# One tile of the memory's keys moved ahead of attention-out, and the slot that it frees loaded first

## What is computed

```
# block 1
merged = gates[0] * (conv_out @ w_conv_out) + gates[1] * (attn_out @ w_attn_out)
x  = x + merged @ w_out
h2 = rms_norm(x, ffn_norm_g)
x  = x + hierarchical_moe(h2, ...)     # 32 experts, each (w_g, w_u, w_d) = 3 x 2 MB
# block 2 (its keys of the memory do not depend on x)
k, v = split(rms_norm_2(mem, g_mem) @ w_kv)
```

## Time and profile before

| | us |
|---|---|
| median of 3 runs (lowest, highest) | 1080.14 (1079.3, 1080.64) |
| the profiled execution, its own time | 1080.13 |
| its span in the trace | 1078.3 |
| busy in the span: TensorE, VectorE, ScalarE | 940.9, 476.3, 346.2 |
| the queue of SyncE's loads | 298.89 MB, 70.3% of 16 engines' span |

### The profile page before, as it was taken

One profiled execution on the slowest core, in us unless ns is written; L12 is line 12 of the kernel. 1 busy time (PEld: TensorE's weight loads), 2 busy tenths in 40 slices (PEclk: granted clock), 3 DMA queues, 4 the chain that ended last, 5 costly groups with the idle time before them and its releaser, 6 DMA issues.

```text
span 1078.3 us, 14213 instructions
## 1 busy us (share of the span) xinstructions
PE 940.9 (87%) x6026; PEld 678.1 (63%) x6026; DVE 476.3 (44%) x774; ACT 346.2 (32%) x558; POOL 1.3 (0%) x5
## 2 busy tenths in 40 slices
PE   6999999999978685867676766889999999999998
PEld 6968888985423141322222131379989999999986
DVE  5769878450101010010101010186865666888842
ACT  5422364131000010000000010247674736665632
POOL 0000000000000000000000000000000000000000
PEclk9999999999989897888888796999999999999999
DMA  8694410699999999999999999972244244556451
GB/s 314 221 370 151 156 40 1 257 395 416 428 421 420 424 427 426 423 429 424 428 422 430 423 427 424 405 253 78 80 154 159 79 157 140 173 179 212 157 195 40
DMA packets 76892, 300.80 MB, mean 279 GB/s; under 512 B 3745, under 2 KB 30498, under 8 KB 60194
## 3 DMA queue, kind: packets, MB, share of 16 engines
q1 hardware_dynamic: 75520, 298.89, 70.3%
q10 hardware_dynamic: 1314, 1.07, 0.3%
HBM read 298.90 MB, written 1.05 MB: 278 GB/s over the span
## 4 chain that ended last, share of the span: by engine, by line
PE 64%; DMA 28%; DVE 5%; ACT 1%; SPq 1%; issue 1%; DVEq 0%; PEldq 0%; ACTq 0%
PE bank L1288 11%; PE bank L647 9%; DMA ring<-in_w_down_e_dram 8%; DMA ring<-in_w_up_e_dram 8%; DMA ring<-in_w_gate_e_dram 8%; PE bank L970 6%; PE bank L1306 6%; PE bank L1174 3%; PE bank L1189 3%; PE bank L734 3%; PE bank L674 3%; PE bank L1081 3%; DMA qvpr<-in_w_down_e_dram 3%; PE bank L1023 3%; PE bank L853 2%; PE bank L995 2%
## 5 line engine op out<-in xcount | busy, mean ns | idle before, releaser
L970 PE MATMUL bank<-ring,big 128*32 128x512 f32 x768 | 165.2, 711 | 64.0 <-DMA ring<-in_w_up_e_dram 37.4
L970 PEld LDWEIGHTS bank<-ring,big 128*32 128x32 f32 x768 | 36.6, 127 | 185.4 <-issue 94.5
L343 DVE TENSOR_TENSOR ring_parts<-ring,ring_parts 128x2048 fp32r<-128x2048 f32 (+1 forms) x54 | 118.8, 2248 | 35.5 <-ACT ring_parts L335 35.2
L335 ACT ACTIVATE ring_parts<-ring 128x2048 fp32r<-128x2048 f32 (+1 forms) x54 | 98.7, 1880 | 48.7 <-DMA ring<-in_w_up_dram 27.0
L970 PE MATMUL bank<-qvpr,big 128*32 128x512 f32 x112 | 64.9, 735 | 23.1 <-DMA qvpr<-in_w_gate_e_dram 11.5
L1288 PE MATMUL bank<-mrg_parts,ring_parts 128*128 128x256 f32 x640 | 82.3, 281 | 0.0
L2025 DVE TENSOR_TENSOR xT<-bank,xT 128x512 f32<-128x512 f32 x32 | 22.1, 691 | 131.3 <-PE bank L1009 131.3
L1288 PEld LDWEIGHTS bank<-mrg_parts,ring_parts 128*128 128x128 f32 x640 | 78.5, 189 | 0.0
L970 PE MATMUL bank<-hs,big 128*32 128x512 f32 x128 | 68.2, 686 | 1.9 <-DMA hs<-in_w_gate_e_dram 1.1
L1979 DVE TENSOR_TENSOR big<-big,const 128x128 f32<-128x128 f32 x16 | 4.1, 290 | 139.3 <-PE bank L957 139.0
L2021 DVE TENSOR_TENSOR big<-bank,big 128x512 f32<-128x512 f32 x8 | 5.5, 691 | 131.1 <-PE bank L970 131.1
(11 more groups left out here) (347 smaller groups left out, 1573.1 us busy)
## 6 DMA issues: line engine op xcount, KB each, us to landing
ring<-in_w_gate_e_dram SPq DMA_DIRECT2D x24, 2048.0 KB, 19.2
ring<-in_w_up_e_dram SPq DMA_DIRECT2D x24, 2048.0 KB, 29.5
ring<-in_w_down_e_dram SPq DMA_DIRECT2D x20, 2048.0 KB, 21.0
ring<-in_w_in_dram SPq DMA_DIRECT2D x13, 2048.0 KB, 13.7
ring<-in_w_up_dram SPq DMA_DIRECT2D x22, 1024.0 KB, 7.1
qvpr<-in_w_down_e_dram SPq DMA_DIRECT2D x5, 2048.0 KB, 25.7
ring<-in_w_down_dram SPq DMA_DIRECT2D x5, 2048.0 KB, 7.9
ring<-in_w_out_dram SPq DMA_DIRECT2D x4, 2048.0 KB, 8.3
```

The costliest lines, as they stand in the source:

```text
L335: signal(act.activation(pairs[stage][u % 3][0][:, part], raws[stage][u % 3][:, part], ACT.Copy), stage + "_hi")
L343: signal(eng.tensor_tensor(lo[:, part], raws[stage][u % 3][:, part], hi[:, part].bitcast(F32), ALU.subtract), name)
L970: mm = pe.matmul(bank[part][CAP * j:CAP * j + CAP, :], xeT[:, c, CAP * j:CAP * j + CAP], w[j][c], start=(c == 0), stop=(c == DC - 1))
```

## The change

Tile 3 of the keys is computed with tiles 0 to 2, ahead of attention-out. Tile 4 takes its old place behind the norm's sum. Nothing stands any more between the transposes and the counting of positions. The semaphore of slot 4, which the first matmul behind tile 3 tells, is so told by the first matmul of attention-out, and SyncE's queue has unit 4 (into slot 4) as its first load. ScalarE's moves follow the tiles, and the list of banks follows the new order.

```
-    ... some("kx", 0, 3) + some("ao", 0, 8) + some("wo", 0, 8)
-    uses += [("n2", 0)] + some("kx", 3, 4) + some("rt", 0, 2) + some("h2t", 0, 4) + some("kx", 4, 5)
+    ... some("kx", 0, 4) + some("ao", 0, 8) + some("wo", 0, 8)
+    uses += [("n2", 0)] + some("kx", 4, 5) + some("rt", 0, 2) + some("h2t", 0, 4)
...
             def first_turn():
+                load_unit(0, 4)
                 load_unit(0, 1)
...
                 load_spare(0)
-                for u in (4, 7):
-                    load_unit(0, u)
+                load_unit(0, 7)
                 sp.wait_ge(S["keys_read"], 1)
                 load_spare(1)
...
-            mem_keys((0, 1, 2))
+            mem_keys((0, 1, 2, 3))
...
             norm_sum(("n2", 0), sq)
-            mem_keys((3,))
+            mem_keys((4,))
...
             freed.append(used[HS])
-            mem_keys((4,))
             pe.wait_ge(S["member"], 1)
...
             # ScalarE
-            for m in range(3):
+            for m in range(4):
                 move(("kx", m), ...)
             arrive(act, ("gt", 15))
             round_out(1)
...
             root(("n2", 0))
-            for m in range(3, 4):
+            for m in range(4, 5):
...
-            for m in range(4, 6):
+            for m in range(5, 6):
```

More of the change, by code:

```diff
@@ L106, in psum_plan @@
     uses += some("gt", 8, 13) + [("mu", 0), ("gt", 13), ("var", 0), ("gt", 14), ("gt", 15)] + some("s1", 4, 8) + some("aT1", 0, 2) + some("co", 0, 4) + some("aT1", 2, 4) + some("mT", 0, 4) + some("o1", 0, 4)
-    uses += some("co", 4, 6) + [("nmem", 0)] + some("on", 0, 2) + some("co", 6, 8) + some("kx", 0, 3) + some("ao", 0, 8) + some("wo", 0, 8)
-    uses += [("n2", 0)] + some("kx", 3, 4) + some("rt", 0, 2) + some("h2t", 0, 4) + some("kx", 4, 5)
+    uses += some("co", 4, 6) + [("nmem", 0)] + some("on", 0, 2) + some("co", 6, 8) + some("kx", 0, 4) + some("ao", 0, 8) + some("wo", 0, 8)
+    uses += [("n2", 0)] + some("kx", 4, 5) + some("rt", 0, 2) + some("h2t", 0, 4)
     uses += some("pos", 0, 2) + [("cnt", 0)] + some("kx", 5, 6)
```

## The result

The changed kernel takes 1087.39 us, the median of six runs (1085.44 to 1088.63), beside 1080.14 for the kernel before (six runs, 1079.3 to 1081.58). The ratio is 1.0067, with a 95% interval of 1.0056 to 1.0078: 7.25 us slower. Timed a second time, beside other kernels, it took 1086.91, ratio 1.0056 (1.0043 to 1.0069). What was expected of the second timing was 1087.4 again, with times spread over 3 us or more if the low clock were a matter of chance; its five times lie between 1086.03 and 1087.46. The forecast was slower by 4.45 us, 1084.6, with its own range of 1083.4 to 1086.0 and an 8-in-10 range of 1082.3 to 1087.5. The sign and the place are right. The time lies outside the first range and only 0.1 us inside the second; the size is near rival 1's, 1087.1.

The account below looks back on a forecast made before the run. It took one DMA stream to bound the experts' stretch. Unit 7, requested 9.0 us later, would land at 247.4 instead of 242.96; those 4.45 us on 1080.13 give 1084.6 us, range 1083.4 to 1086.0 (8 in 10: 1082.3 to 1087.5).

Parts of the forecast that it names:

- rival 1: Clock low through the counting and tile 5; unit 7 goes at 239.2; delay 7.0 us, 1087.1 us; chance 0.12.
- The stream is the bound, and lateness passes whole: Experts' stretch: one DMA stream bounds it; moving its end moves the kernel's end by as much; 4.45 us pass whole.
- By as much: Behind the experts' stream: whatever moves the stream's end moves the kernel's end by the same amount.
- The tile ahead of attention-out fills no wait: Three tiles already cover attention-out's wait to within 0.5 us; the fourth puts everything dependent back by 3.45 us.
- The pause, and slot 6 told by tile 5: Ahead of the counting: TensorE pauses 3.8 us; tile 5 tells slot 6, unit 7 goes 9.0 us later, gap 6 us.
- the sum: At unit 7's landing: 247.4 against 242.96 us, 4.45 us later, passed whole to the end: 1084.6 us.
- unit 4's bytes: Unit 4's early load, 2 MiB, takes 4.9 us out of the stream; the gap before unit 7 is longer.
- The price of the clock: Half clock after the pause: 0.5 us taken for the counting, 1 us more for tile 5 of 0 to 3.5.
- So no further gap: Behind unit 7: second spare half goes at 242.9, stream busy until 245.2, so later loads come in time.
- The landing of a lone load: Unit 7, alone in an idle queue, lands 8.8 us after its request, as the load of w_out did.

Follow-up runs that it names:

- the run with the old queue: The changed kernel with unit 4's load back at its old place in the queue, the changed order on TensorE kept: 1087.03 us, ratio 1.0054.
- the run with the pause filled: The changed kernel with eight empty matmuls of 256 columns between the transposes and the counting: 1084.88 us, ratio 1.0041; again 1085.08, ratio 1.0042.
- the kernel with only the shift: The kernel before with eight empty matmuls of 256 columns, 3.45 us, ahead of attention-out: 1083.89 us, ratio 1.0030.

## Why the prediction came out as it did

**The stream is the bound, and lateness passes whole: right.** 3.45 us of empty matmuls cost 3.3 us in the median. "By as much" holds to within 1.5 us in a single execution, since behind the stream one block takes 6.0 or 7.5 us by the clock that it meets.

**The tile ahead of attention-out fills no wait: right.** Its block has no pause, and the counting begins 3.45 us later in the second profile, start taken off, as foretold. In the first it is 5.0 us, of which 0.70 are the start, 3.45 the tile, and the rest slow logits and transposes.

**The pause, and slot 6 told by tile 5: right; the gap was larger than 6 us.** The stream stands still at 236 to 242 us. By the sum's own counting the gap is 8.0 us (from 221.08 + 1.6 + 12.3 to 243.0), and 7.3 us in the second profile. That unit 4's bytes are not gained is shown by the run with the old queue.

**The price of the clock: the term that was too small.** The sum had 0.5 us for the counting, nothing for the telling of slot 6 at a low clock, and nothing ahead of the pause. Measured, start taken off:

| | the sum | second profile | first profile |
|---|---|---|---|
| late ahead of the counting, beyond 3.45 us | 0 | 0 | 0.85 |
| the counting, beyond 1.14 us | 0.5 | 1.0 | 1.0 |
| from tile 5's start to the request of unit 7 | 0.63 | 1.23 | 1.24 |
| unit 7 asked for | 238.6 | 239.7 | 240.6 |
| lateness of the stream at unit 7's last byte | 4.5 | 5.8 | 6.6 |
| lateness of the stream's end | 4.5 | 6.9 | 7.7 |

Unit 7 asked for 1.1 to 2.0 us later than in the sum is the larger part of the miss of 2.8 us.

**"So no further gap": wrong by a little.** Tile 5 was given 1 us more and took 2.0 and 2.3. The second spare half went at 245.3 and 244.8 without the start, not at 242.9, just as unit 7's bytes ran out; the sag there costs 0.3 to 0.6 us. The last 0.6 to 0.7 us of the stream's lateness no run takes apart.

**Rival 1**, to which I gave 0.12, has the mechanism: the clock low all through the counting and most of tile 5. That its 7.0 us is also the size is in part luck. It asked for unit 7 at 239.2, too early, and had a second gap of 1.9 us, too long. With the full clock the forecast nearly holds, in a kernel that has eight more matmuls: the run with the pause filled took 1084.88 and 1085.08 us in the median against 1084.1 to 1084.6 expected, and the stream of its profile at full clock ends 4.5 us late, start taken off. The error was to take low or middle values of the clock's price, where both profiles of the changed kernel show nearly the whole of it for the counting, more than half for tile 5, and 0.6 us for the telling matmul. The fall ahead of the pause, in the first profile, comes on top.

**The landing of a lone load** was put at 8.8 us and was 7.7 and 7.8. It made the sum by landings 1.1 us too large and hid a part of the other error.

## What to carry to other kernels

Where a stream of loads bounds a stage, look at when each slot is told free and by which instruction, not at where the program says that it is: moving a tile here took away the matmul that told slot 6. Taking bytes out of the stream early was worth nothing while the next request was late. When a filler is removed and a pause is left (3.8 us here), price everything behind it that gates a load at half the clock, the telling matmul too. Profile a changed kernel twice before its size is explained: the first profile alone would have laid the loss to a low clock ahead of the pause, and the second is nearly as slow without it.

## What the runs showed of the hardware

- **The low clock came without a pause, too.** In the first profile of the kernel after, and in the kernel with only the shift, TensorE had had no pause since the keys' tiles when the granted clock fell to 0.50: it was 1.00 over 227 to 230 us and 0.50 from 231, during the router's matmuls of 36 columns. With the shift alone it was 0.50 over 231 to 237 with TensorE busy for 6.00 of 6.00 us:

```profile
231.00:237.00 6.00, 6.00 (x26) 5.69 (x26) 4.17 (x26) 3.96 (x5) 0.00 (x0) 0.50 1.01 431
```

- **The same matmuls don't bring it each time.** The kernel before ran the logits and transposes at 1.00 (3.66 and 1.94 us), and so did the second profile of the kernel after, where the low clock came with the pause instead. The kernel with the pause filled showed it in one profile and not in the other. In the first profile of the kernel after it lasted from 231 to 244 us, in the second it was 0.50 over 237 to 243. What decides in which execution it comes stays open; no run here tells.
- **Small matmuls pay it almost in full.** The logits took 3.66 us at full clock and 7.01 at half, the transposes 1.94 and 3.65, the counting 1.14 and 2.15.
- **A restart of the stream** costs what it did in the kernel before, where full rate counted from 1.6 to 1.7 us after the request. For unit 7 in the kernel after it is 243.0 against the request at 241.28, and 1.9 us in the second profile.
